# Expert stage of a hybrid encoder layer: all weight low parts on VectorE, casts on ScalarE, three pairs of gate/up banks, expert loop written out

## The chip, the cores and the metric

The kernel runs on one core of a Trainium2 chip. The metric is the device time of one execution in microseconds (us), as the median of several runs. Beside the timed runs there is one profiled execution, from which all rows below come. The core has five engines that run their own instruction lists and meet only at semaphores: PE (TensorE, matrix products), DVE (VectorE), ACT (ScalarE), POOL (GpSimd) and SP (SyncE, which here only issues DMAs).

## What is computed

One encoder layer over 1,024 prompt tokens and 256 sample tokens of width 1,024. The first part (normalisation, projections, neighbourhood attention, Fourier mixing, gated merge) is untouched. The change concerns the second part, an expert-choice feed-forward layer: each of 16 experts picks its top tokens (128 of the prompt, 32 of the sample, 160 together), applies a gated unit of width 2,048, and adds the weighted rows back.

```python
def expert_choice_ffn(h, w_router, w_gate_e, w_up_e, w_down_e):
    cap = EC_CAPACITY_FACTOR * N // N_EXPERTS
    aff = jax.nn.softmax((h @ w_router).astype(jnp.float32), axis=-1)
    gates, idx = lax.top_k(aff.T, cap)
    xe = h[idx]
    def one_expert(args):
        xc, wg, wu, wd = args
        a = xc @ wg
        b = xc @ wu
        return (jax.nn.silu(a) * b) @ wd
    ye = lax.map(one_expert, (xe, w_gate_e, w_up_e, w_down_e))
    ye = ye * gates[..., None].astype(ye.dtype)
    return jnp.zeros_like(h).at[idx.reshape(-1)].add(ye.reshape(-1, D))
```

## The kernel before

**Numbers in two parts.** To keep fp32 accuracy every fp32 operand is split into a high part (`w_hi`, `x_hl[..., 0, :]`, `act_hl[..., 0, :]`, type fp32r, written by ACT) and a low part, the difference (`w_lo` in bf16; `x_hl[..., 1, :]`, `act_hl[..., 1, :]` in fp32r). A product of weights with tokens is then `w_hi` times both parts of the tokens (320 columns: 160 high, 160 low; line 1621) plus `w_lo` times a bf16 copy of the tokens, `x_b` or `act_b` (160 columns, line 1624), summed in the same PSUM bank.

**Tiles.** Weights of an expert arrive in 12 chunks of 2 MB in four `raw` slots (line 557, issued by SP). A chunk holds two units; a unit is 2,048 numbers per partition. An expert has 24 units: 0 to 15 for gate and up, 16 to 23 for down. ACT writes the high part of a unit (line 911), then DVE or POOL its low part (`low_part`, line 459): POOL the units with v % 3 == 2 (`POOLS`, eight per expert), DVE the other sixteen (`DVES`). Six unit slots hold them. High parts run four units ahead of the products (`ahead`).

**PE's order for one expert** (the loop at line 1643): 16 gate/up tiles j, each of two half-tiles (gate, up) of 8 + 8 matmuls, into a pair of PSUM banks; then the transposes of the next expert's tokens (lines 1611 and 1612); then eight down products d of 16 + 16 matmuls, each followed by the turning back of the product before (`back`, lines 1659 and 1660); then tile 0 of the next expert, and the last turning back. Gate/up tiles alternate between two bank pairs, so tile j waits until tile j-2 has been taken out:

```python
for j in range(1, FT):
    if j >= 2:
        pe.wait_ge(gu_added, e * FT + (j - 1))
    tile_of_gate_and_up(e, j)
```

**Taking a tile out**: ACT copies the low sums from PSUM (`lows`, line 929); DVE adds them to the high sums (`gu`, line 1276, which signals `gu_added`); ACT forms `silu` (line 936); DVE multiplies (`act_f`, line 1283). For every two tiles ACT writes the high part of the result (line 940), and DVE its bf16 copy `act_b` (line 1289) and its low part (line 1291). In the down stage DVE also scales the next expert's tokens (`x_f`, line 980), casts them to `x_b` (line 1260), forms their low part (line 1264), adds `yT` (line 1298) and scales the finished rows (lines 1305 and 1306).

**POOL** also gathers the next expert's rows and adds the finished rows to the output by indirect DMAs (lines 731, 733, 760, 762).

Every engine runs its list in the order written; in the expert stage that list stands once in a loop over 16 experts, with wait values computed in registers from the loop's counter.

Of the kernel before, what the change touches and what calls it, by code (L numbers as in the profile page):

```python
# [30 lines left out]
ACT = mybir.ActivationFunctionType  # L31
# [20 lines left out]
EXPERTS, FF = 16, 2048  # L52
FT = FF // P
# [40 lines left out]

POOLS = [v for v in range(UNITS) if v % 3 == 2]
DVES = [v for v in range(UNITS) if v % 3 != 2]

# [13 lines left out]
TILES = attention_tiles()  # L111
X_BANKS = ((6, 0, 3), (7, 3, 3), (0, 6, 2))
Y_BANKS = ((1, 2), (6, 7))


def build(nc, x, g1, w_in, q_g, k_g, rpb, w_na, w_fo, w_out, g2, w_r, w_g, w_u, w_d,
          dft_c, pos_c, pos_s, spos_c, spos_s, col_mask, y):
    ctx = ExitStack()
    with ctx:
# [282 lines left out]
        hi_ready = sem("hi_ready")  # L402
        lo_dve = sem("lo_dve")
        lo_pool = sem("lo_pool")
        first_units = sem("first_units")
# [6 lines left out]
        x_hi_ready = sem("x_hi_ready")  # L412
        x_ready = sem("x_ready")
        gu_ready = sem("gu_ready")
        low_ready = sem("low_ready")
# [24 lines left out]
        def wait_split(engine, e, v):  # L440

            if v in POOLS:
                engine.wait_ge(lo_pool, e * len(POOLS) + (POOLS.index(v) + 1))
            else:
                engine.wait_ge(lo_dve, e * len(DVES) + (DVES.index(v) + 1))

# [19 lines left out]
        def _(sp):  # L466
# [130 lines left out]
            sp.wait_ge(first_units, LEAD)  # L597
            with sp.Fori(0, EXPERTS - 1) as e:
                for c in range(CHUNKS_E):
                    wait_chunk_split(e, c)  # L600
                    n = c + RAW_SLOTS
                    expert_load(e + n // CHUNKS_E, n % CHUNKS_E)
# [14 lines left out]
        def _(pool):  # L617
# [97 lines left out]

            pool.sem_inc(lo_pool, sum(v in POOLS for v in range(LEAD)))
            for v in range(LEAD):
# [18 lines left out]

            def lows(e, step):
                for v in ahead(step):
                    if v % UNITS in POOLS:
                        low_part(pool, e, v, lo_pool)  # L740

            gather(0)
            with pool.Fori(0, EXPERTS) as e:
                lows(e, 0)
                pool.wait_ge(x_tr, e + 1)
                gather(e + 1)
                for step in range(1, 4):
                    lows(e, step)
                pool.wait_ge(rows_moved, e * 64 + 64)
                pool.tensor_copy(idx_scatter[:, :], idx_t[:, :, bass.ds(e, 1)].rearrange("p a b -> p (a b)"))\  # L750
                    .then_inc(sc_count, 1)
                pool.tensor_copy(gate_now[:, :], gate_t[:, :, bass.ds(e, 1)].rearrange("p a b -> p (a b)"))\
                    .then_inc(sc_count, 1)
                pool.wait_ge(sc_count, e * 2 + 2)
                pool.sem_inc(cols_ready, 1)
                for step in range(4, 16):
                    lows(e, step)
                pool.wait_ge(y_ready, e * 4 + 5)
                apart(pool, pool_passed)
                pool.indirect_dma_start(y, bass.IndirectOffsetOnAxis(idx_scatter[:, 0:1], 0), ye_p[:, :], None,  # L760
                                        compute_op=ALU.add).then_inc(rows_moved, 16)
                pool.indirect_dma_start(y, bass.IndirectOffsetOnAxis(idx_scatter[0:CAP_S, 1:2], 0),
                                        ye_s[:, :], None, compute_op=ALU.add).then_inc(rows_moved, 16)
# [4 lines left out]
        def _(act):  # L768
# [148 lines left out]
            def token_high(n):  # L917
                act.wait_ge(xf_ready, n + 1)
                act.activation(x_hl[:, :, 0, :], x_f[:, :, :], ACT.Copy).then_inc(x_hi_ready, 1)

            token_high(0)
            with act.Fori(0, EXPERTS) as e:
                def low_sums(j):

                    b = 2 * (j % 2)
                    act.wait_ge(gu_ready, e * FT + (j + 1))
# [45 lines left out]
        def _(dve):  # L972
            dve.sem_inc(o_out, 1)
            dve.sem_inc(m_mul, 6)
            dve.sem_inc(lo_dve, sum(v in DVES for v in range(LEAD)))
            dve.sem_inc(y_ready, 1)
# [275 lines left out]
            def expert_tokens(n):  # L1252
# [15 lines left out]
            token_low(0)  # L1268
            with dve.Fori(0, EXPERTS) as e:
                def split(v):  # L1270
                    if v % UNITS in DVES:
                        low_part(dve, e, v, lo_dve)

                def add_lows(j):
                    dve.wait_ge(low_ready, e * FT + (j + 1))
                    dve.tensor_tensor(gu[j % 2][:, :, :], gate_up(2 * (j % 2))[:, :, 0:CAP], lows[j % 2][:, :, :],  # L1276
                                      ALU.add).then_inc(gu_added, 1)

                def gated_up(j):
                    dve.wait_ge(silu_ready, e * FT + (j + 1))  # L1280
                    if j >= 4 and j % 2 == 0:
                        dve.wait_ge(act_hi_ready, e * 8 + (j // 2 - 1))
                    dve.tensor_tensor(act_f[j // 2 % 2][:, j % 2, :], silu[j % 2][:, :], gu[j % 2][:, 1, :],  # L1283
                                      ALU.mult).then_inc(act_f_ready, 1)

                def act_low(pair):
                    pairs = slice(2 * pair, 2 * pair + 2)
                    dve.wait_ge(act_f_ready, e * FT + (2 * pair + 2))
                    dve.tensor_copy(act_b[:, pairs, :], act_f[pair % 2][:, :, :])  # L1289
                    dve.wait_ge(act_hi_ready, e * 8 + (pair + 1))  # L1290
# [48 lines left out]
        def _(pe):  # L1339
# [288 lines left out]
            def tile_of_gate_and_up(e, j):  # L1628
                b = 2 * (j % 2)
                for n in range(2):  # L1630
# [9 lines left out]
            pe.wait_ge(first_units, LEAD)  # L1640
            pe.wait_ge(x_ready, 1)
            tile_of_gate_and_up(0, 0)
            with pe.Fori(0, EXPERTS) as e:
# [19 lines left out]
                for d in range(KT):  # L1663
# [67 lines left out]
```

## Time and profile before

| | |
|---|---|
| time, median of 3 runs | 2791.22 us (2789.4 to 2794.93) |
| profiled execution | 2797.54 us, span 2795.7 us |
| PE busy | 2556.1 us, 91% of the span |
| DVE busy | 1766.6 us, 63% |
| ACT busy | 1250.2 us, 45% |
| POOL busy | 942.4 us, 34% |
| mean granted TensorE clock | 0.959 of full speed |

The shares mix two stages. Up to about 1,180 us DVE and POOL are lightly used; from there to the end, in the expert stage, PE and DVE are both busy some nine tenths of the time. An engine that is busy is not by that alone the one that sets the time: it has to be seen who waits for whom, and for how long.

### The profile page before, as it was taken

How to read it: one execution, taken by the hardware profiler on the slowest of the kernel's cores; microseconds unless marked ns; L12 is line 12 of the kernel's file. 1: busy time of each engine (PE TensorE's matmuls, PEld its weight loads, DVE VectorE, ACT ScalarE, POOL GpSimd, SP SyncE). 2: the span in 40 equal slices, each digit the busy share in tenths (PEclk: the TensorE clock that was granted, in tenths of full speed). 3: DMA queues.
4: the chain of work that ended last, by engine and by line, in shares of the span. 5: the costliest groups of instructions: out<-in, count | busy, mean ns of one | idle time of the engine just before them, and what ended most of it. 6: DMA issues, size and time to landing. Idle time of an engine off the chain costs nothing.

```text
span 2795.7 us, 46497 instructions
## 1 busy us (share of the span) xinstructions
PE 2556.1 (91%) x17866; PEld 2176.0 (78%) x17866; DVE 1766.6 (63%) x2096; ACT 1250.2 (45%) x1720; POOL 942.4 (34%) x364
## 2 busy tenths in 40 slices
PE   6989999999999999299999998999999999999997
PEld 5876776767767687188888888888888888889886
DVE  5114234231010233698898889889889988988986
ACT  4123333230000111166666566566666656656664
POOL 4130110101111000245445444535544554453553
PEclk7999999999999999599999999999999999999999
DMA  4240101100110153277878778778787787877872
GB/s 135 46 90 8 36 8 21 38 0 26 41 45 23 64 192 133 95 251 260 275 255 275 272 240 289 252 257 278 259 275 254 266 281 240 291 257 245 283 259 69
DMA packets 338433, 481.07 MB, mean 172 GB/s; under 512 B 22090, under 2 KB 194521, under 8 KB 338400
## 3 DMA queue, kind: packets, MB, share of 16 engines
q1 hardware_dynamic: 331072, 455.05, 48.0%
q0 software_dynamic: 7328, 25.58, 4.0%
q8 instruction: 21, 0.34, 0.1%
q14 instruction: 12, 0.10, 0.0%
HBM read 455.73 MB, written 24.87 MB: 172 GB/s over the span
## 4 chain that ended last, share of the span: by engine, by line
PE 57%; issue 24%; DVE 15%; ACT 3%; POOL 0%; DVEq 0%; DMA 0%; SPq 0%; ACTq 0%; POOLq 0%
PE ps L1343 26%; PE ps L1621 13%; PE ps L1624 6%; DVE act_f L1283 4%; PE ps L1544 4%; PE ps L1469 3%; DVE gu L1276 2%; DVE w_lo L459 2%; PE ps L1482 2%; DVE act_b L1289 1%; DVE act_hl L1291 1%; ACT w_hi L911 1%; DVE x_b L1260 1%; DVE x_f L980 1%; PE ps L1431 1%
## 5 line engine op out<-in xcount | busy, mean ns | idle before, releaser
L459 POOL TENSOR_TENSOR w_lo<-raw,w_hi 128x2048 bf16<-128x2048 f32 x132 | 643.1, 4873 | 745.7 <-ACT w_hi L911 745.4
L1621 PE MATMUL ps<-x_hl,w_hi 128*128 128x320 f32 x4112 | 746.3, 325 | 102.5 <-DVE gu L1276 97.9
L911 ACT ACTIVATE w_hi<-raw 128x2048 fp32r<-128x2048 f32 x388 | 739.3, 1906 | 3.0 <-issue 2.9
L1621 PEld LDWEIGHTS ps<-x_hl,w_hi 128*128 128x128 f32 x4112 | 620.7, 193 | 119.0 <-DVE gu L1276 71.7
L459 DVE TENSOR_TENSOR w_lo<-raw,w_hi 128x2048 bf16<-128x2048 f32 x256 | 621.1, 2426 | 79.3 <-ACT w_hi L911 79.3
L1624 PE MATMUL ps<-x_b,w_lo 128*128 128x160 bf16 x4112 | 380.8, 237 | 0.0
L1621 PE MATMUL ps<-act_hl,w_hi 128*128 128x320 f32 x2048 | 343.6, 319 | 0.0
L1624 PEld LDWEIGHTS ps<-x_b,w_lo 128*128 128x128 bf16 x4112 | 277.9, 99 | 53.8 <-issue 2.8
L1621 PEld LDWEIGHTS ps<-act_hl,w_hi 128*128 128x128 f32 x2048 | 306.2, 191 | 1.8
L1283 DVE TENSOR_TENSOR act_f<-silu,gu 128x160 f32<-128x160 f32 x256 | 290.5, 1135 | 19.4 <-ACT silu L936 19.4
L1291 DVE TENSOR_TENSOR act_hl<-act_f,act_hl 128x320 fp32r<-128x320 f32 x128 | 200.4, 1565 | 7.1 <-ACT act_hl L940 7.1
L1107 DVE TENSOR_TENSOR mT<-sig,ps 128x512 f32 (+1 forms) x24 | 14.4, 599 | 273.8 <-PE ps L1343 273.8
L929 ACT ACTIVATE lows<-ps 128x320 f32<-128x320 f32 x256 | 110.9, 433 | 142.8 <-PE ps L1624 141.3
L1624 PE MATMUL ps<-act_b,w_lo 128*128 128x160 bf16 x2048 | 171.9, 235 | 0.0
L884 ACT ACTIVATE sig<-ps 128x512 f32<-128x512 f32 (+1 forms) x48 | 25.3, 527 | 316.5 <-PE ps L1343 316.5
L1343 PE MATMUL ps<-hx_hi,w_high 128*128 128x512 f32 (+1 forms) x672 | 154.6, 373 | 7.3 <-POOL w_low L654 4.8
L936 ACT ACTIVATE silu<-gu 128x160 f32<-128x160 f32 x256 | 85.7, 335 | 160.0 <-DVE gu L1276 160.0
L1624 PEld LDWEIGHTS ps<-act_b,w_lo 128*128 128x128 bf16 x2048 | 140.3, 99 | 16.7 <-issue 0.8
L1343 PE MATMUL ps<-hx_lo,w_high 128*128 128x512 f32 (+1 forms) x672 | 142.2, 354 | 0.0
L1343 PE MATMUL ps<-hx_hi,w_low 128*128 128x512 f32 (+1 forms) x672 | 142.1, 354 | 0.0
L1343 PEld LDWEIGHTS ps<-hx_hi,w_high 128*128 128x128 f32 x672 | 114.5, 190 | 34.3 <-issue 11.1
L698 POOL CAST w_high<-m_raw 128x1024 fp32r<-128x1024 f32 x16 | 16.7, 1041 | 351.4 <-PE ps L1343 306.5
(189 smaller groups left out, 3053.5 us busy)
## 6 DMA issues: line engine op xcount, KB each, us to landing
raw<-in_w_g SPq DMA_DIRECT2D x64, 2048.0 KB, 8.1
raw<-in_w_u SPq DMA_DIRECT2D x64, 2048.0 KB, 9.9
raw<-in_w_d SPq DMA_DIRECT2D x64, 2048.0 KB, 8.4
m_raw<-in_w_in SPq DMA_DIRECT2D x16, 512.0 KB, 4.4
h_raw<-in_w_in SPq DMA_DIRECT2D x12, 512.0 KB, 4.1
x_in<-in_x SPq DMA_DIRECT2D x10, 512.0 KB, 4.1
x_res<-in_x SPq DMA_DIRECT2D x10, 512.0 KB, 4.0
y_out<-x SPq DMA_DIRECT2D x10, 512.0 KB, 2.9
```

What stands on the lines that cost most here:

```text
L459: engine.tensor_tensor(unit(w_lo, v), raw_half(v), unit(w_hi, v).bitcast(F32), ALU.subtract)\
L911: act.activation(unit(w_hi, w), raw_half(w), ACT.Copy).then_inc(hi_ready, 1)
L929: act.activation(lows[j % 2][:, :, :], gate_up(b)[:, :, CAP:2 * CAP], ACT.Copy)\
L936: act.activation(silu[j % 2][:, :], gu[j % 2][:, 0, :], ACT.Silu).then_inc(silu_ready, 1)
L1276: dve.tensor_tensor(gu[j % 2][:, :, :], gate_up(2 * (j % 2))[:, :, 0:CAP], lows[j % 2][:, :, :], ALU.add).then_inc(gu_added, 1)
L1283: dve.tensor_tensor(act_f[j // 2 % 2][:, j % 2, :], silu[j % 2][:, :], gu[j % 2][:, 1, :], ALU.mult).then_inc(act_f_ready, 1)
L1291: dve.tensor_tensor(act_hl[:, pairs, 1, :], act_f[pair % 2][:, :, :], act_hl[:, pairs, 0, :].bitcast(F32), ALU.subtract).then_inc(act_read ...
L1343: op = pe.matmul(out, lhsT, rhs, start=n == 0, stop=n == len(pairs) - 1)
L1469: op = pe.matmul(ps[:, at0:at0 + n], qkvT[part, 0, P * t:P * t + P], qkvT[part, 1, key0:key0 + n], start=True, stop=True)
L1544: op = pe.matmul(bank(2 * u + half), tokens[u][:, k, :], weights[:, k, BANK * half:BANK * half + BANK], start=k == 0 and n == 0, stop=k == ...
L1621: pe.matmul(out, unit(w_hi, v)[:, k, cols], hl[:, k, :, :].rearrange("p a n -> p (a n)"), start=k == 0, stop=False)
L1624: op = pe.matmul(out[:, CAP:2 * CAP], unit(w_lo, v)[:, k, cols], b[:, k, :], start=False, stop=k == n - 1)
```

## The change

- The low parts of all 24 units of an expert are made by DVE; POOL makes none in the loop (it still makes the first four units before it). One semaphore, `lo_ready`, takes the place of `lo_dve` and `lo_pool`.
- The bf16 copies `x_b` and `act_b` are made by ACT, right behind the high parts, in place of DVE; two new semaphores, `xb_ready` and `act_b_ready`, tell PE and DVE of them.
- Gate/up tiles go round three bank pairs (`GU_BANKS`), so tile j waits for tile j-3; the transposes and the turned rows move to other banks, and PE's wait for the finished rows of the expert before moves from ahead of the transposes to ahead of tile 2.
- The loops over the experts on all five engines are written out, so that waits are on constants.

```diff
-X_BANKS = ((6, 0, 3), (7, 3, 3), (0, 6, 2))
-Y_BANKS = ((1, 2), (6, 7))
+X_BANKS = ((6, 0, 3), (7, 3, 3), (2, 6, 2))
+Y_BANKS = ((3, 0), (6, 7))
+GU_BANKS = (0, 2, 6)
...
         def wait_split(engine, e, v):
-            if v in POOLS:
-                engine.wait_ge(lo_pool, e * len(POOLS) + (POOLS.index(v) + 1))
-            else:
-                engine.wait_ge(lo_dve, e * len(DVES) + (DVES.index(v) + 1))
+            engine.wait_ge(lo_ready, e * UNITS + (v + 1))
...
-            with sp.Fori(0, EXPERTS - 1) as e:
+            for e in range(EXPERTS - 1):
...
-            with pool.Fori(0, EXPERTS) as e:
-                lows(e, 0)
+            for e in range(EXPERTS):
                 pool.wait_ge(x_tr, e + 1)
                 gather(e + 1)
-                for step in range(1, 4):
-                    lows(e, step)
...
-                for step in range(4, 16):
-                    lows(e, step)
...
                 act.activation(x_hl[:, :, 0, :], x_f[:, :, :], ACT.Copy).then_inc(x_hi_ready, 1)
+                act.activation(x_b[:, :, :], x_f[:, :, :], ACT.Copy).then_inc(xb_ready, 1)
...
-                    b = 2 * (j % 2)
+                    b = GU_BANKS[j % 3]
...
                        .then_inc(act_hi_ready, 1)
+                    act.activation(act_b[:, 2 * pair:2 * pair + 2, :], act_f[pair % 2][:, :, :], ACT.Copy)\
+                       .then_inc(act_b_ready, 1)
...
-                dve.wait_ge(xf_ready, n + 1)
-                dve.tensor_copy(x_b[:, :, :], x_f[:, :, :])
...
                 def split(v):
-                    if v % UNITS in DVES:
-                        low_part(dve, e, v, lo_dve)
+                    low_part(dve, e, v, lo_ready)
...
-                        dve.wait_ge(act_hi_ready, e * 8 + (j // 2 - 1))
+                        dve.wait_ge(act_b_ready, e * 8 + (j // 2 - 1))
...
-                    dve.tensor_copy(act_b[:, pairs, :], act_f[pair % 2][:, :, :])
...
-                    if j >= 2:
-                        pe.wait_ge(gu_added, e * FT + (j - 1))
+                    if j == 2:
+                        pe.wait_ge(y_ready, e * 4 + 1)
+                    if j >= 3:
+                        pe.wait_ge(gu_added, e * FT + (j - 2))
                     tile_of_gate_and_up(e, j)
                 pe.wait_ge(gu_added, e * FT + (FT - 1))
-                pe.wait_ge(y_ready, e * 4 + 1)
...
                             pe.wait_ge(act_ready, e * 8 + k1 // 2)
+                            pe.wait_ge(act_b_ready, e * 8 + k1 // 2)
...
                 pe.wait_ge(x_ready, e + 2)
+                pe.wait_ge(xb_ready, e + 2)
```

What that moves on the engines is seen best in their instruction lists. First DVE at two tiles in the middle of the gate/up stage (`gu` and `act_f` take a tile out, `w_lo` is the low part of a unit, `act_hl` the low part of the result); before:

```order
L1276 TENSOR_TENSOR gu_198<-ps,lows_200 128x320
L1283 TENSOR_TENSOR act_f_196<-silu_206,gu_198 128x160
L1275 REGISTER_ALU
L1276 TENSOR_TENSOR gu_197<-ps,lows_199 128x320
L457 REGISTER_ALU
L459 TENSOR_TENSOR w_lo_187<-raw_171,w_hi_181 128x2048
L1289 CAST act_b<-act_f_196 128x320
L1290 REGISTER_ALU
L1291 TENSOR_TENSOR act_hl<-act_f_196,act_hl 128x2x160
L1283 TENSOR_TENSOR act_f_195<-silu_205,gu_197 128x160
```

and in the changed kernel:

```order
L1262 TENSOR_TENSOR gu_198<-ps,lows_200 128x320
L456 TENSOR_TENSOR w_lo_184<-raw_172,w_hi_178 128x2048
L1269 TENSOR_TENSOR act_f_195<-silu_206,gu_198 128x160
L1262 TENSOR_TENSOR gu_197<-ps,lows_199 128x320
L456 TENSOR_TENSOR w_lo_185<-raw_173,w_hi_179 128x2048
L1276 TENSOR_TENSOR act_hl<-act_f_195,act_hl 128x2x160
L1269 TENSOR_TENSOR act_f_196<-silu_205,gu_197 128x160
```

Behind every `gu` there is now a `w_lo` of DVE's own, and the cast and the register instructions are gone. Second, PE at tiles 1 to 3 (`w_hi` times `x_hl` is the high product, `w_lo` times `x_b` the low one; a wait stands behind the instruction that has it); before:

```order
L443 ISA [waits gu_added]
L1621 MATMUL ps<-x_hl,w_hi_180 128x320 [waits lo_pool]
L1621 MATMUL ps<-x_hl,w_hi_180 128x320 x7
L1624 MATMUL ps<-x_b,w_lo_186 128x160 x8
L445 REGISTER_ALU
L1621 MATMUL ps<-x_hl,w_hi_181 128x320 [waits lo_dve]
L1621 MATMUL ps<-x_hl,w_hi_181 128x320 x7
L1624 MATMUL ps<-x_b,w_lo_187 128x160 x8
L1646 REGISTER_ALU
L1621 MATMUL ps<-x_hl,w_hi_180 128x320 [waits gu_added]
```

and in the changed kernel:

```order
L1606 MATMUL ps<-x_hl,w_hi_180 128x320 [waits lo_ready,y_ready]
L1606 MATMUL ps<-x_hl,w_hi_180 128x320 x7
L1609 MATMUL ps<-x_b,w_lo_186 128x160 x8
L1606 MATMUL ps<-x_hl,w_hi_181 128x320 [waits lo_ready]
L1606 MATMUL ps<-x_hl,w_hi_181 128x320 x7
L1609 MATMUL ps<-x_b,w_lo_187 128x160 x8
L1606 MATMUL ps<-x_hl,w_hi_180 128x320 [waits gu_added]
```

Tile 2 no longer waits for `gu_added` but for the finished rows (`y_ready`); the wait for `gu_added` begins at tile 3, and it is for tile 0. The products themselves are the same.

## Rows read from the trace of the kernel before

**Rows 1.** Busy us of PE, PEld, DVE, ACT, POOL by stretch; PEclk, DMA share, GB/s

```profile
1443.57:2742.62 1299.05, 1215.44 (x10403) 1125.26 (x10401) 1150.24 (x1054) 799.47 (x949) 619.22 (x195) 0.98 0.78 264
1493.53:1499.78 6.25, 5.31 (x33) 5.01 (x34) 5.85 (x8) 3.20 (x5) 5.03 (x5) 0.73 1.00 366
```

**Rows 2.** PE's transposes (line 1611) in first and last expert: first, last start

```profile
L1611 PE MATMUL ps<-ident,xg_p x8: 273/327/328, 1245.0 to 1247.9; 128*128 128x128 f32 x8
...
L1611 PE MATMUL ps<-ident,xg_p x8: 272/328/328, 2742.6 to 2745.6; 128*128 128x128 f32 x8
```

**Rows 3.** Timeline of PE: start us, duration us, line, count, [idle before <-releaser]

```profile
1186.13 1.41 PE L1621 MATMUL ps<-x_hl,w_hi 128*128 128x320 f32 x8
...
1427.97 1.43 PE L1621 MATMUL ps<-x_hl,w_hi 128*128 128x320 f32 x8 [0.47 <-DVE gu L1276]
...
1436.90 1.42 PE L1621 MATMUL ps<-x_hl,w_hi 128*128 128x320 f32 x8
1438.16 0.73 PE L1624 MATMUL ps<-x_b,w_lo 128*128 128x160 bf16 x8
1439.95 1.43 PE L1621 MATMUL ps<-x_hl,w_hi 128*128 128x320 f32 x8 [1.06 <-DVE gu L1276]
...
1446.98 2.03 PE L1621 MATMUL ps<-act_hl,w_hi 128*128 128x320 f32 x12
...
1450.63 2.59 PE L1621 MATMUL ps<-act_hl,w_hi 128*128 128x320 f32 x16
...
1454.89 0.33 PE L1659 MATMUL ps<-ident,yT 128*128 128x128 f32 x1 [0.56 <-DVE yT L1298]
...
1455.09 2.59 PE L1621 MATMUL ps<-act_hl,w_hi 128*128 128x320 f32 x16
...
1480.97 1.42 PE L1621 MATMUL ps<-x_hl,w_hi 128*128 128x320 f32 x8
...
1494.47 1.43 PE L1621 MATMUL ps<-x_hl,w_hi 128*128 128x320 f32 x8 [2.59 <-DVE gu L1276]
```

**Rows 4.** Waits of PE, whole run: us in total, times, longest us

```profile
PE ps L1621 <- DVE gu L1276: 97.9, 80, 2.6
...
PE ps L1659 <- DVE yT L1298: 6.1, 11, 0.6
```

**Rows 5.** Timeline of POOL, then of DVE, at one of those waits

```profile
1487.94 5.82 POOL L459 TENSOR_TENSOR w_lo<-raw,w_hi 128x2048 bf16<-128x2048 f32 x1
...
1489.27 4.67 DVE L1283 TENSOR_TENSOR act_f<-silu,gu 128x160 f32<-128x160 f32 x1
```

**Rows 6.** DVE by line: ns min/median/max; page's groups: count | busy, mean ns

```profile
L1283 DVE TENSOR_TENSOR act_f<-silu,gu x256: 306/311/5248, 1189.4 to 2745.7; 128x160 f32<-128x160 f32 x128
...
L1283 DVE TENSOR_TENSOR act_f<-silu,gu 128x160 f32<-128x160 f32 x256 | 290.5, 1135 | 19.4 <-ACT silu L936 19.4
...
L1291 DVE TENSOR_TENSOR act_hl<-act_f,act_hl x128: 475/478/4848, 1199.7 to 2746.5; 128x320 fp32r<-128x320 f32 x128
...
L1291 DVE TENSOR_TENSOR act_hl<-act_f,act_hl 128x320 fp32r<-128x320 f32 x128 | 200.4, 1565 | 7.1 <-ACT act_hl L940 7.1
...
L459 DVE TENSOR_TENSOR w_lo<-raw,w_hi x256: 2268/2274/4246, 1187.2 to 2774.9; 128x2048 bf16<-128x2048 f32 x128
...
L1260 DVE CAST x_b<-x_f x17: 828/5083/5085, 1177.4 to 2748.6; 128x1280 bf16<-128x1280 f32 x17
```

**Rows 7.** ACT by line, 1,300 to 2,700 us: count | busy, mean ns

```profile
L911 ACT ACTIVATE w_hi<-raw 128x2048 fp32r<-128x2048 f32 x337 | 642.4, 1906 | 2.8 <-issue 2.8
...
L929 ACT ACTIVATE lows<-ps 128x320 f32<-128x320 f32 x225 | 97.5, 433 | 123.4 <-PE ps L1624 122.0
...
L940 ACT ACTIVATE act_hl<-act_f 128x320 fp32r<-128x320 f32 x112 | 52.4, 468 | 99.5 <-DVE act_f L1283 99.5
```

**Rows 8.** Instruction-loading queue: packets, MB, share; whole run, then 1180.26 to 1245.0 us

```profile
q8 instruction: 21, 0.34, 0.1%
...
q8 instruction: 4, 0.07, 0.4%
```

More of the change, by code:

```diff
@@ L92, in ahead @@
     return [2 * step + LEAD, 2 * step + LEAD + 1] if step < 8 else [step + 8 + LEAD]
-POOLS = [v for v in range(UNITS) if v % 3 == 2]
-DVES = [v for v in range(UNITS) if v % 3 != 2]
 def attention_tiles():
@@ L402, in build @@
         hi_ready = sem("hi_ready")
-        lo_dve = sem("lo_dve")
-        lo_pool = sem("lo_pool")
+        lo_ready = sem("lo_ready")
         first_units = sem("first_units")
@@ L413, in build @@
         x_ready = sem("x_ready")
+        xb_ready = sem("xb_ready")
+        act_b_ready = sem("act_b_ready")
         gu_ready = sem("gu_ready")
@@ L714, in _ @@
             pool.wait_ge(anti_ready, 2)
-            pool.sem_inc(lo_pool, sum(v in POOLS for v in range(LEAD)))
             for v in range(LEAD):
@@ L735, in gather @@
                     .then_inc(rows_moved, 16)
[L737 to L740, printed above, removed]
             gather(0)
-            with pool.Fori(0, EXPERTS) as e:
-                lows(e, 0)
+            for e in range(EXPERTS):
                 pool.wait_ge(x_tr, e + 1)
                 gather(e + 1)
-                for step in range(1, 4):
-                    lows(e, step)
                 pool.wait_ge(rows_moved, e * 64 + 64)
@@ L919, in token_high @@
                 act.activation(x_hl[:, :, 0, :], x_f[:, :, :], ACT.Copy).then_inc(x_hi_ready, 1)
+                act.activation(x_b[:, :, :], x_f[:, :, :], ACT.Copy).then_inc(xb_ready, 1)
             token_high(0)
-            with act.Fori(0, EXPERTS) as e:
+            for e in range(EXPERTS):
                 def low_sums(j):
-                    b = 2 * (j % 2)
+                    b = GU_BANKS[j % 3]
                     act.wait_ge(gu_ready, e * FT + (j + 1))
@@ L974, in _ @@
             dve.sem_inc(m_mul, 6)
-            dve.sem_inc(lo_dve, sum(v in DVES for v in range(LEAD)))
+            dve.sem_inc(lo_ready, LEAD)
             dve.sem_inc(y_ready, 1)
@@ L1268, in _ @@
             token_low(0)
-            with dve.Fori(0, EXPERTS) as e:
+            for e in range(EXPERTS):
                 def split(v):
-                    if v % UNITS in DVES:
-                        low_part(dve, e, v, lo_dve)
+                    low_part(dve, e, v, lo_ready)
                 def add_lows(j):
                     dve.wait_ge(low_ready, e * FT + (j + 1))
-                    dve.tensor_tensor(gu[j % 2][:, :, :], gate_up(2 * (j % 2))[:, :, 0:CAP], lows[j % 2][:, :, :],
+                    dve.tensor_tensor(gu[j % 2][:, :, :], gate_up(GU_BANKS[j % 3])[:, :, 0:CAP], lows[j % 2][:, :, :],
                                       ALU.add).then_inc(gu_added, 1)
@@ L1628, in tile_of_gate_and_up @@
             def tile_of_gate_and_up(e, j):
-                b = 2 * (j % 2)
+                b = GU_BANKS[j % 3]
                 for n in range(2):
@@ L1641, in _ @@
             pe.wait_ge(x_ready, 1)
+            pe.wait_ge(xb_ready, 1)
             tile_of_gate_and_up(0, 0)
-            with pe.Fori(0, EXPERTS) as e:
+            for e in range(EXPERTS):
                 for j in range(1, FT):
-                    if j >= 2:
-                        pe.wait_ge(gu_added, e * FT + (j - 1))
+                    if j == 2:
+                        pe.wait_ge(y_ready, e * 4 + 1)
+                    if j >= 3:
+                        pe.wait_ge(gu_added, e * FT + (j - 2))
                     tile_of_gate_and_up(e, j)
                 pe.wait_ge(gu_added, e * FT + (FT - 1))
-                pe.wait_ge(y_ready, e * 4 + 1)
                 pe.wait_ge(rows_moved, e * 64 + 64)
```

## Prediction

> **What bounds the kernel now.** I read first the busy time by stretch. In the 1,299 us from the third expert's transposes to the last one's PE is busy 94%, DVE 89%, ACT 62%, POOL 48%, and the DMA engines 78% [rows 1]. So PE is nearest to its limit, with DVE close behind, and the question is what PE does in the missing time.
>
> Then the distance of the experts: PE's transposes, once per expert, start at 1245.0 and, 15 experts later, at 2742.6 [rows 2]: 99.84 us each.
>
> Then PE's own work for one expert, from its timeline where it does not wait [rows 3]. Five half-tiles in a row take 1436.90 - 1427.97 = 8.93 us, 1.786 each, so 3.572 a tile and 57.15 for 16 tiles. The transposes end where the down products begin: 1446.98 - (1439.95 + 3.57) = 3.46. The first down product takes 1450.63 - 1446.98 = 3.65, the second 1454.89 - 0.56 of waiting - 1450.63 = 3.70. From 1455.09 to 1480.97 lie the other six, their turnings back and tile 0: 25.88 - 3.57 = 22.31. The sum is **90.27 us**, 9.57 less than the distance.
>
> Then PE's waits [rows 4]: 97.9 us in 80 waits for `gu`, five per expert, 6.1 us per expert. Each costs more than its idle time, since the next products would have begun under the tail of the last ones: 0.52 us after 1438.16 (half-tile of 1.786, less the 1.26 from 1436.90), and they began at 1439.95, 1.27 late for a wait of 1.06 [rows 3]. That is 0.2 x 5 = 1.0 us. After the longest wait (2.59 us, at 1494.47) the granted clock of the next 6.25 us is 0.73, and over the whole stretch 0.98 [rows 1, 3]; with levels of 1.2 and 2.4 GHz, 0.73 means 54% of 6.25 us at the lower one, 1.7 us lost. The wait for `yT` (11 times, 0.56 + 0.2) adds 0.5. Together 9.3 of the 9.57 us.
>
> Last, why DVE is late with `gu`. Its neighbour in the list, `act_f`, takes 0.31 us in the median but 4.67 at 1489.27, and it ends 0.2 us after a low part of POOL (1487.94 + 5.82 = 1493.76) [rows 5]. The mean is 1135 ns against a median of 311; `act_hl` 1565 against 478; the cast to `x_b` 5083 against 828 at its fastest [rows 6]. So DVE stands still while POOL subtracts, and per expert that is (1135 - 311) x 16 = 13.2, (1565 - 478) x 8 = 8.7 and 4.3: 26.2 us.
>
> **The change part by part.**
>
> *POOL's eight low parts go to DVE.* Added: 8 x 2.27 = 18.2 us per expert (the median, and within 6 ns the minimum, so this operation alone takes no longer [rows 6]). Removed: the 26.2 us of standing still, 0.83 for the `x_b` cast, and eight small casts. DVE is busy 1150.24 / 13 experts = 88.5 us now; I get 88.5 + 18.2 - 26.2 - 0.8, about 80, of 90.27: below PE. Where it is tightest, in the gate/up stage, DVE has for two tiles two low parts (4.54), two `act_f` (0.62), one `act_hl` (0.48) and two `gu` (as large as `act_hl`, 0.96): 6.6 us, while PE takes 7.14. That fits, with half a microsecond to spare per two tiles.
>
> *Casts to ACT.* `act_b` has the shape of the high part beside it, 0.47 us [rows 7]. For two tiles ACT has two high parts (3.81), two `lows` (0.87), two `silu` (smaller than `lows`, at most 0.87), and two casts of 0.47: 6.5 of 7.14 us at most. The `x_b` cast is smaller than a unit's high part (1.91); it lies in the down stage, where ACT has one high part per product of 3.7 us. No cost: its cover is ACT's idle time (62% busy [rows 1]); without it the cost would be 8 x 0.47 + 1.9 = 5.7 us per expert.
>
> *Three bank pairs.* A tile must be out by the end of the tile after next, 7.14 us after its own end, in place of 3.57. Without POOL's interference it is out, at the latest, after `lows` (0.43), a low part that DVE has just begun (2.27) and the add (0.48): 3.2 us. Two pairs would just do; with three nearly 4 us are in hand. So all five waits per expert go, with the clock's fall behind the longest of them. What is late next: `yT` of the first down product, behind which PE waits 0.56 now. In its path the 5.1 us `x_b` cast goes and a low part of 2.27, which must wait for ACT's high part, comes in. From the end of the last tile (T): `lows`, `gu`, `silu`, `act_f` and the last high part of the result, 0.43 + 0.48 + 0.43 + 0.31 + 0.47 = 2.1 us, or 4.4 if a low part stands ahead; then `act_b` 0.47, the unit's high part 1.91, its low part 2.27, three `x_f` of together some 1.7 (estimate: twice the fastest `x_b`, which has as many elements) and `yT` 0.31: T + 8.8 to T + 11.1. PE asks for it at T + 3.46 + 3.65 + 3.70 = T + 10.8. Mostly in time: I count this wait as gone, and up to 0.5 us per expert in the range.
>
> *The wait for the finished rows moves* to tile 2. Queued behind it are all later tiles; behind the last turning back PE has tile 1 (3.57 us) to do, while DVE scales two pieces of 512 columns (1.7 us by the fastest `x_b`, which has 1,280). No cost. PE's new waits on `act_b` and `x_b` end with casts that ACT makes beside DVE's low part of the same numbers.
>
> *The loop written out.* Of the 22.31 us above, six down products of 3.65 leave 0.4 for seven turnings back and the loop's end together [rows 3], so the loop costs PE at most that, 6 us in all; I take nothing. In its place about 28,700 instructions of PE are loaded in place of 4,700. Now 21 packets bring 0.34 MB in the whole run [rows 8]; then some 127. In the first expert four came in while PE went from tile 1 at 1186.13 to its transposes at 1245.0, 58.87 us: 5.3 above its 15 tiles' 53.58, where the mean expert loses 9.57. Loading is hidden there. I take nothing; the price, if not, is a rival.
>
> The Trainium skill's page "Runtime: NRT & Kernel Launch", section "Instruction fetch mechanics", says that a taken branch out of the window at hand stalls until the target has been fetched, which is why full unrolling is preferred. By it the written-out loop would bring a gain of its own at each of 15 loop ends, one fetch long; by the row it is at most 0.4 us each. The sum is 2642 by the row and could be 2636 by the rule.
>
> *DMA.* 0.78 x 99.84 = 77.9 us of transfers per expert [rows 1]; 90.27 us hold them, at 86%.
>
> *Sum.* First expert, from tile 1 to the transposes: 5.3. Fifteen distances: 15 x 9.57 = 143.6. The last down stage: 0.7 for its `yT`. Together **149.6 us**, which makes the profiled 2797.5 a 2647.9; the median of the runs is 6.3 us (0.2%) below the profiled run, so I forecast 2791.2 - 149.6 = **2642 us**.
>
> **The rivals.**
>
> *PE keeps waiting a little for DVE.* DVE's reserve is half a microsecond in two tiles and less at the first `yT`; the in-order lists of ACT and DVE hang on each other, and a hiccup of one is worked off slowly. For: the thin sums above. Against: the third bank pair. A microsecond per expert is 16 us, three are 48: 2658 to 2690.
>
> *DVE is not freed.* If its long `act_f` have another cause than POOL, it has 88.5 + 18.2 - 5.1 for `x_b`, less eight small casts (0.48 at most), 98 to 102 us per expert, as many as PE has now: no change, about 2790. Against: the end of the long one falls on POOL's [rows 5].
>
> *Slower: instruction loading.* The 106 further packets come through DMA engines that are then 86% busy. If each holds up PE for 1.4 us, the 149.6 us are gone, and beyond that the kernel is slower: at 3 us each, 2642 + 318 = 2960. For: nothing in this trace loads code steadily beside such traffic. Against: the first expert [rows 8].
>
> *Slower: ACT and DVE in step.* If DVE's low part kept ACT from the next tile, a tile would take 0.43 + 1.91 + 2.27 + 0.31 = 4.92 us; it decides from (99.84 - 33.1) / 16 = 4.2. At 4.92 an expert takes 111.8: about 2985. Against: in ACT's list nothing waits for `w_lo`.
>
> **How the numbers follow.** PE without waits, 2632 to 2652: 0.80. Small waits left, up to 2690: 0.12. No change: 0.02. Loading: 0.04. In step: 0.02. The range reaches over the first two, 2632 to 2690. A measurement tells about 0.2% from no change; faster 0.92, same 0.02, slower 0.06.
>
> **What would show it.** Transposes every 90.3 us; PE's wait for `gu` gone; granted clock 1.0 in the expert stage; means of `act_f` and `act_hl` at their medians; DVE some 80 us per expert. Wrong if PE idles at regular places with no engine as releaser (loading), if `yT` of the first down product shows on PE, or if DVE's low parts take more than 2.27 us: from 2.27 + (90.27 - 80) / 24 = 2.7 us each DVE is the bound.

## The result and the profile after

The changed kernel takes 2660.9 us (median of 4 runs, 2658.1 to 2664.1) beside 2791.6 us for the kernel before: a ratio of 0.953, with a 95% interval of 0.951 to 0.954. On another chip, with five runs, it was 2659.8 us, and 0.951 (0.950 to 0.952). The forecast was 2642, the range 2632 to 2690. The sign and most of the size are right; 19 us of the forecast gain are missing. Two executions far outside the others, one of the kernel before (3119.3 us) and one of the closer mixture below (6312.6 us), are left out of all ratios.

The profiled execution took 2658.06 us. First its busy time by engine, then the expert stage by stretch, from the first expert's transposes to the last one's (columns as in [rows 1]):

```profile
PE 2520.9 (95%) x17866; PEld 2159.3 (81%) x17866; DVE 1558.9 (59%) x2079; ACT 1302.0 (49%) x1865; POOL 419.3 (16%) x236
```

```profile
1238.50:2602.60 1364.10, 1364.10 (x12003) 1277.53 (x12001) 1130.67 (x1201) 970.17 (x1230) 232.55 (x105) 0.99 0.88 292
```

PE is busy for all of the 1364.1 us, where it had 94% before [rows 1]. DVE has 1130.67 / 15 = 75.4 us per expert, where it had 88.5, though it makes eight more low parts.

Of the waits [rows 4] nothing is left. From the first expert's first product to the end, PE's list has one row, the start of the stage, which the kernel before had too:

```profile
PE ps L1606 <- DVE x_hl L1251: 4.6, 1, 4.6
```

DVE by line, 1,330 to 2,580 us (count, busy us, mean ns, idle before), which answers to [rows 6]:

```profile
L456 DVE TENSOR_TENSOR w_lo<-raw,w_hi 128x2048 bf16<-128x2048 f32 x329 | 751.5, 2287 | 159.3 <-ACT w_hi L897 158.7
...
L1269 DVE TENSOR_TENSOR act_f<-silu,gu 128x160 f32<-128x160 f32 x218 | 69.1, 317 | 5.6 <-ACT silu L923 5.6
L1276 DVE TENSOR_TENSOR act_hl<-act_f,act_hl 128x320 fp32r<-128x320 f32 x109 | 52.9, 485 | 8.5 <-ACT act_hl L927 8.5
```

The means of `act_f` and `act_hl` are now where their medians were: 317 ns for 1135, 485 for 1565.

The chain of work that ended last, once 57% PE and 24% "issue", is PE alone, and code is loaded in 116 packets in place of 21 [rows 8]:

```profile
PE 93%; DVE 3%; issue 1%; ACT 1%; POOL 1%; DMA 0%; SPq 0%; DVEq 0%; ACTq 0%; POOLq 0%
...
q8 instruction: 116, 1.90, 0.3%
```

If PE never waits, where are the missing 19 us? The transposes, which answer to [rows 2], lie 90.2 us apart in eight of the 15 distances and 91.7 or 91.8 in seven. Three of them in a row of experts (first and last start in us):

```profile
L1596 PE MATMUL ps<-ident,xg_p x8: 273/327/328, 1509.2 to 1512.1; 128*128 128x128 f32 x8
...
L1596 PE MATMUL ps<-ident,xg_p x8: 272/327/328, 1599.4 to 1602.4; 128*128 128x128 f32 x8
...
L1596 PE MATMUL ps<-ident,xg_p x8: 273/327/328, 1691.1 to 1694.1; 128*128 128x128 f32 x8
```

The first distance is 90.2, the second 91.7. By stretch (PEclk is the third last column): the transposes at 1599.4, the 5.2 us behind them, and the same place one expert earlier:

```profile
1599.40:1602.81 3.41, 3.41 (x19) 2.11 (x16) 2.56 (x5) 1.19 (x4) 0.00 (x0) 0.99 0.95 319
1602.81:1608.00 5.19, 5.19 (x34) 4.78 (x33) 3.43 (x4) 2.22 (x3) 0.00 (x0) 0.68 1.01 375
1509.20:1515.00 5.80, 5.80 (x38) 4.40 (x37) 3.19 (x7) 3.41 (x5) 0.00 (x0) 1.00 1.00 346
```

Behind the transposes of some experts the granted clock is 0.68, with no idle time of PE before: between the levels of 1.2 and 2.4 GHz that is 64% of 5.19 us at the lower one, 1.7 us lost, and a whole expert that is 1.5 us longer. All seven long experts have this fall, in this place (0.67 to 0.71); the others do not (1.00). Why these seven and not the others is open.

### The profile page after: what moved, and what is told of

The parts are those of the page before. It is cut to its first block, busy times and chain, and to the rows that moved or that the text cites. A ratio compares the mean times of both kernels' runs of the same rounds, so it can differ in the third digit from the quotient of the medians.

```text
span 2656.3 us, 44107 instructions
## 1 busy us (share of the span) xinstructions
PE 2520.9 (95%) x17866; PEld 2159.3 (81%) x17866; DVE 1558.9 (59%) x2079; ACT 1302.0 (49%) x1865; POOL 419.3 (16%) x236
## 4 chain that ended last, share of the span: by engine, by line
PE 93%; DVE 3%; issue 1%; ACT 1%; POOL 1%; DMA 0%; SPq 0%; DVEq 0%; ACTq 0%; POOLq 0%
PE ps L1606 35%; PE ps L1328 27%; PE ps L1609 17%; PE ps L1529 4%; PE ps L1454 3%; PE ps L1467 2%; PE ps L1596 1%; PE ps L1597 1%; PE ps L1416 1%; PE ps L1646 1%; PE ps L1647 1%; PE ps L1374 0%; DVE top_i L1212 0%; DVE aff L1214 0%; DVE top_v L1211 0%
## 5 line engine op out<-in xcount | busy, mean ns | idle before, releaser
L456 DVE TENSOR_TENSOR w_lo<-raw,w_hi 128x2048 bf16<-128x2048 f32 x384 | 877.2, 2287 | 186.8 <-ACT w_hi L897 186.2
L1606 PE MATMUL ps<-x_hl,w_hi 128*128 128x320 f32 x4112 | 730.2, 320 | 4.6 <-DVE x_hl L1251 4.6
L1606 PEld LDWEIGHTS ps<-x_hl,w_hi 128*128 128x128 f32 x4112 | 607.8, 189 | 5.1 <-issue 4.7
L1609 PE MATMUL ps<-x_b,w_lo 128*128 128x160 bf16 x4112 | 374.1, 234 | 0.0
L1609 PEld LDWEIGHTS ps<-x_b,w_lo 128*128 128x128 bf16 x4112 | 272.2, 98 | 52.7 <-issue 0.2
L746 POOL DMA_INDIRECT y_out<-ye_p,idx_scatter x16 | 83.1, 5196 | 1105.4 <-DVE ye_s L1291 1105.4
L1328 PEld LDWEIGHTS ps<-hx_lo,w_high 128*128 128x128 f32 x672 | 113.4, 190 | 18.0
L1328 PEld LDWEIGHTS ps<-hx_hi,w_low 128*128 128x128 f32 x672 | 113.0, 189 | 17.5
L1262 DVE TENSOR_TENSOR gu<-ps,lows 128x320 f32<-128x320 f32 x256 | 123.3, 482 | 5.7 <-ACT lows L916 5.7
L936 ACT ACTIVATE y_low<-ps 128x160 f32<-128x160 f32 x128 | 38.9, 304 | 178.3 <-PE ps L1609 178.3
```

Of the source, the lines that this page charges most:

```text
L456: engine.tensor_tensor(unit(w_lo, v), raw_half(v), unit(w_hi, v).bitcast(F32), ALU.subtract)\
L936: act.activation(y_low[d % 2][:, :], bank(4 + d % 2, CAP, first=CAP), ACT.Copy)\
L1262: dve.tensor_tensor(gu[j % 2][:, :, :], gate_up(GU_BANKS[j % 3])[:, :, 0:CAP], lows[j % 2][:, :, :], ALU.add).then_inc(gu_added, 1)
L1328: op = pe.matmul(out, lhsT, rhs, start=n == 0, stop=n == len(pairs) - 1)
L1606: pe.matmul(out, unit(w_hi, v)[:, k, cols], hl[:, k, :, :].rearrange("p a n -> p (a n)"), start=k == 0, stop=False)
L1609: op = pe.matmul(out[:, CAP:2 * CAP], unit(w_lo, v)[:, k, cols], b[:, k, :], start=False, stop=k == n - 1)
```

## The experiments

Eleven runs tell three things apart: which of the four parts of the change brought the gain, why POOL's work had cost so much, and what the remaining 1.5 us are. The ratios are against the kernel before on the same chip: its median is 2795.1 us beside the changed kernel once more, the run without the written-out loop, the one with two bank pairs and the transposes laid between; 2794.6 beside the runs with all low parts on DVE, with three bank pairs and with idle work on POOL; 2793.8 beside the casts on ACT, the closer mixture and the two things together.

### The changed kernel once more

> The changed kernel once more, beside the runs below on the same chip, as the level that they are held against. The theory: PE alone sets the time of an expert (90.24 us of its own work in the trace of the changed kernel, and no waits), and in 7 of 15 experts 1.5 us more at a lower granted clock right behind the transposes. Expected: 2661 us, within 4, and again some experts at 90.2 and some at 91.7 us.

Measured: 2659.8 us (2653.5 to 2662.0), ratio 0.951 (0.950 to 0.952); seven experts again at 91.7 or 91.8 us, the same seven in the order of experts, and eight at 90.2.

### The change without the written-out loop

```diff
-            for e in range(EXPERTS):
+            with pe.Fori(0, EXPERTS) as e:
                 for j in range(1, FT):
```

and likewise on the other four engines.

> The changed kernel with its five expert loops put back as loops. Theory (the loop's end costs PE at most 0.4 us per expert): 2661 to 2667 us, and only one expert's code loaded. Rival (a branch back costs the fetch of its target, so writing out the loop was part of the gain): a gap on PE at each of 15 loop ends, of 1 us or more, 2676 us and above. A second rival (the steady loading of code costs the changed kernel something): below 2655 us.

Measured: 2661.3 us, ratio 0.952 (0.951 to 0.953), the same as the change. PE has no gap at a loop's end, and 21 packets load code in the whole run in place of 116. The written-out loop neither brings nor costs anything that can be measured.

### The change with two bank pairs

```diff
-                b = GU_BANKS[j % 3]
+                b = GU_BANKS[j % 2]
...
-                    if j == 2:
-                        pe.wait_ge(y_ready, e * 4 + 1)
-                    if j >= 3:
-                        pe.wait_ge(gu_added, e * FT + (j - 2))
+                    if j >= 2:
+                        pe.wait_ge(gu_added, e * FT + (j - 1))
```

with `GU_BANKS = (0, 2)`, `X_BANKS` and `Y_BANKS` as before, and the wait for the finished rows ahead of the transposes again.

> The changed kernel with two pairs of gate/up banks as before. Theory (POOL's low parts held up DVE, and without them a tile is out 3.2 us after its end, with 3.57 allowed): 2661 to 2672 us, no more than small waits of PE for gu. Rival (the third pair is what freed PE): PE's waits for gu come back, five per expert at 1 us or more, 2735 us and above.

Measured: 2657.1 us, ratio 0.951 (0.949 to 0.952). PE does not wait once in the expert stage. With all low parts on DVE the third pair is not needed.

### The kernel before, with all low parts on DVE and nothing else

```diff
-POOLS = [v for v in range(UNITS) if v % 3 == 2]
-DVES = [v for v in range(UNITS) if v % 3 != 2]
+POOLS = []
+DVES = list(range(UNITS))
...
-            pool.sem_inc(lo_pool, sum(v in POOLS for v in range(LEAD)))
```

> The kernel before, with one thing changed: DVE makes all 24 low parts, POOL none. Casts stay on DVE, two bank pairs, the loop stays. Theory (DVE stood still while POOL subtracted): act_f and act_hl fall to 0.31 and 0.48 us in the mean, DVE has 88.5 + 18.2 - 26.2 = 80.5 us per expert, PE 90.3; little waiting is left: 2661 to 2700 us. Rival (the third bank pair or the casts are needed for the gain, DVE has too much to do): PE's waits for gu stay at several us per expert, 2740 us and above.

Measured: 2660.2 us, ratio 0.952 (0.950 to 0.955): the whole gain of the change, with two bank pairs, the casts on DVE and the loop. PE has no waits, and the cast that took 5.1 us is back at its fastest (DVE by line, 1,330 to 2,580 us):

```profile
L1282 DVE TENSOR_TENSOR act_f<-silu,gu 128x160 f32<-128x160 f32 x217 | 68.5, 316 | 5.6 <-ACT silu L935 5.6
...
L1259 DVE CAST x_b<-x_f 128x1280 bf16<-128x1280 f32 x14 | 11.6, 827 | 0.5
```

DVE has as many low parts to make as in the changed kernel, and the casts besides, and is still busy for only 1069.87 us of 1,250, PE for all of them:

```profile
1330.00:2580.00 1250.00, 1250.00 (x10961) 1170.72 (x10961) 1069.87 (x1218) 840.42 (x996) 232.40 (x98) 0.99 0.86 289
```

### The kernel before, with three bank pairs and nothing else

```diff
-                    b = 2 * (j % 2)
+                    b = GU_BANKS[j % 3]
...
-                    if j >= 2:
-                        pe.wait_ge(gu_added, e * FT + (j - 1))
+                    if j == 2:
+                        pe.wait_ge(y_ready, e * 4 + 1)
+                    if j >= 3:
+                        pe.wait_ge(gu_added, e * FT + (j - 2))
...
-                pe.wait_ge(y_ready, e * 4 + 1)
```

with the bank tables of the change, and the same `b` where ACT and DVE take a tile out.

> The kernel before, with one thing changed: three pairs of gate/up banks. POOL keeps its eight low parts, the casts stay on DVE, the loop stays. Theory: DVE still stands still 26 us per expert, but its 88.5 us are under PE's 90.3, so with 7.14 us in place of 3.57 to take a tile out most of the waits for gu are hidden, the one for yT stays (0.76 us): 2680 to 2740 us. Rival (standing still costs PE whatever the banks allow, since the low parts come late too): 2780 us and above. Rival the other way (the third pair alone is the gain): 2665 us or below.

Measured: 2811.0 us, ratio 1.007 (1.005 to 1.008), a little slower than before. My theory (2740 at the most) missed; the time is in the range of the first rival (2780 and above), but not for its reason: for low parts that come late PE waits 3.2 us in the whole stage. PE's waits from 1,180 us on (us in total, times, longest us; line 1612 is a transpose, 1622 a tile):

```profile
PE ps L1612 <- DVE gu L1277: 61.9, 16, 3.9
PE ps L1622 <- DVE gu L1277: 30.1, 31, 1.5
PE ps L1622 <- POOL w_lo L460: 3.2, 15, 0.2
```

Between the tiles the third pair does what it is for: 30 us of waits in place of 98 [rows 4]. But DVE is no faster for it. It falls behind over the whole gate/up stage, and the transposes behind the last tile, which wait for tile 14's `gu`, then stand for all of it at once, 3.9 us in each expert. My expectation had taken DVE's 88.5 us of the whole expert against PE's 90.3. The stage decides. In one gate/up stage up to the transposes, with PE at 52.66 us, DVE has work or stands for 56.72 of 58.70:

```profile
1385.50:1444.20 58.70, 52.66 (x466) 48.71 (x465) 56.72 (x52) 37.68 (x51) 33.11 (x12) 1.00 0.89 296
```

More buffers hide a lateness that comes and goes, not one that adds up.

PE's waits are 95 us together, 9 less than before [rows 4], and the kernel is 16 us slower even so. What PE loses besides is clock: behind the long wait in each expert come the small transposes, and the granted clock is low there, 0.65 over 9.8 us in the expert below. From the third expert's transposes to the last one's it is 0.96, where it was 0.98 [rows 1]; 0.02 of some 1,300 us is 26 us.

```profile
1443.00:2752.00 1309.00, 1229.76 (x10400) 1131.39 (x10400) 1154.42 (x1056) 791.71 (x951) 628.86 (x195) 0.96 0.78 263
1444.20:1454.00 9.80, 9.80 (x49) 7.46 (x49) 9.16 (x12) 3.17 (x5) 3.35 (x1) 0.65 0.99 356
```

One of DVE's stops in this kernel, POOL's instruction and DVE's:

```profile
1435.40 4.61 POOL L460 TENSOR_TENSOR w_lo<-raw,w_hi 128x2048 bf16<-128x2048 f32 x1 [6.63 <-ACT w_hi L912]
1435.58 4.61 DVE L1290 CAST act_b<-act_f 128x320 bf16<-128x320 f32 x1
```

The victim here is the small cast, which was never held in the kernel before (327 ns at the most): whichever such instruction comes next while POOL subtracts.

### The kernel before, with the casts on ACT and nothing else

```diff
                 act.activation(x_hl[:, :, 0, :], x_f[:, :, :], ACT.Copy).then_inc(x_hi_ready, 1)
+                act.activation(x_b[:, :, :], x_f[:, :, :], ACT.Copy).then_inc(xb_ready, 1)
...
                 op.then_inc(xf_ready, 1)
-                dve.wait_ge(xf_ready, n + 1)
-                dve.tensor_copy(x_b[:, :, :], x_f[:, :, :])
...
                     dve.wait_ge(act_f_ready, e * FT + (2 * pair + 2))
-                    dve.tensor_copy(act_b[:, pairs, :], act_f[pair % 2][:, :, :])
```

and `act_b` on ACT behind its high part, with the waits of the change.

> The kernel before with one thing changed: the casts to x_b and act_b on ACT. POOL keeps its low parts, two bank pairs, the loop stays. Theory: the 5.1 us of x_b leave DVE in the down stage, where PE waits 0.76 us for yT in 11 of 16 experts; in the gate/up stage another two-operand instruction of DVE meets POOL's low parts, so PE's five waits for gu stay: 2770 to 2795 us. Rival (the casts were what made DVE late): below 2740 us.

Measured: 2796.4 us, ratio 1.001 (1.000 to 1.002): nothing, and 1 us above the range of my theory. The cast `x_b` has left DVE, and the next instruction takes its place as the victim. First DVE's low part of the tokens, 1.48 us when it is alone, then PE's waits:

```profile
L1267 DVE TENSOR_TENSOR x_hl<-x_f,x_hl 128x1280 fp32r<-128x1280 f32 x13 | 73.4, 5645 | 0.0
```

```profile
PE ps L1623 <- DVE gu L1279: 76.9, 66, 2.6
PE ps L1662 <- DVE yT L1300: 28.9, 16, 1.9
```

The waits for `gu` are fewer (97.9 before), those for `yT` more (6.1 before).

### The changed kernel, with idle work on POOL

Two kernels give POOL work again at the eight places per expert where it had made low parts. It goes to a buffer of its own that nobody reads. The first subtracts, from two SBUF operands; the second only fills.

```diff
+                        for n in range(3):
+                            pool.wait_ge(junk_done, count[0])
+                            pool.tensor_tensor(junk[:, :, :], src, src, ALU.subtract).then_inc(junk_done, 1)
```

```diff
+                        for n in range(6):
+                            pool.wait_ge(junk_done, count[0])
+                            pool.memset(junk[:, :, :], 0.0).then_inc(junk_done, 1)
```

> The changed kernel, and POOL given work again that nobody needs: at the eight places per expert where it made low parts, three subtractions of 640 numbers each from two SBUF operands, written to a buffer of its own. Theory (POOL's subtractions hold DVE's two-operand instructions): act_f and act_hl are in the mean well above 0.31 and 0.48 us again, DVE has 75 + some 20 to 25 us per expert, over PE's 90.2, and PE waits again: 2720 to 2830 us. Rival (the long DVE instructions had another cause, such as the weights' own low parts on POOL reading the raw slots): act_f at 0.31 us, 2661 us.

Measured: 2869.4 us in a single run, 75 above the kernel before. POOL's and DVE's groups and PE's waits:

```profile
L743 POOL TENSOR_TENSOR junk<-ident 128x640 bf16<-128x640 f32 x384 | 811.7, 2114 | 610.2 <-ACT w_hi L915 587.7
```

```profile
L457 DVE TENSOR_TENSOR w_lo<-raw,w_hi 128x2048 bf16<-128x2048 f32 x288 | 754.5, 2623 | 78.0 <-ACT w_hi L915 78.0
L1287 DVE TENSOR_TENSOR act_f<-silu,gu 128x160 f32<-128x160 f32 x192 | 142.7, 743 | 4.8 <-ACT silu L941 4.8
...
L1294 DVE TENSOR_TENSOR act_hl<-act_f,act_hl 128x320 fp32r<-128x320 f32 x96 | 84.2, 877 | 7.3 <-ACT act_hl L945 7.3
```

```profile
PE ps L1614 <- DVE gu L1280: 60.7, 15, 4.6
PE ps L1624 <- DVE gu L1280: 48.2, 35, 2.3
PE ps L1664 <- DVE yT L1301: 26.0, 15, 1.7
```

Work on data that has nothing to do with the weights makes PE wait at all three places, the tiles, the transposes and `yT`; `act_f` is at 743 ns for 317. So the raw slots and the semaphores of the low parts were not the cause. It cost more than I expected (2830 at the most): a subtraction of 640 took 2.1 us, three of them 6.3 at each place, where one low part had taken 4.9.

> As the run before, but POOL fills the buffer (six fills of 640 numbers at each place) and reads nothing. If only POOL work that reads SBUF holds DVE, as the Trainium skill's page on SBUF has it for DVE instructions with two SBUF operands: act_f at 0.31 us, about 2661 us. If any POOL work does: act_f above 0.31 us in proportion to the time of the fills, 2670 us and above.

Measured: 2662.9 us in a single run, as the changed kernel. POOL is busy 882 us in all, more than twice the 419 of the changed kernel, and DVE does not notice (the page's group of POOL, then DVE by line):

```profile
L742 POOL MEMSET junk<- 128x640 bf16 x768 | 493.1, 642 | 640.6 <-ACT w_hi L914 602.1
```

```profile
L1286 DVE TENSOR_TENSOR act_f<-silu,gu 128x160 f32<-128x160 f32 x216 | 68.4, 317 | 5.6 <-ACT silu L940 5.6
```

Of the two kinds of work on POOL, the one that reads SBUF holds DVE and the one that only writes it does not; that it is the reading, and not another difference between a subtraction and a fill, these two runs alone do not show. The Trainium skill's page "SBUF — State Buffer", section "Who interferes with whom", says this: a DVE instruction with two SBUF inputs contends with a GpSimd instruction that reads SBUF, not with one that only writes it, and the later one waits out the whole of the earlier. Both runs agree (743 ns against 317), and so does `gu`, which has one operand in PSUM and was at 477 ns beside POOL's subtractions. By the runs two inputs are not needed, though: the casts read one operand, in SBUF, and were held as well, `x_b` for 5083 ns in place of 828 [rows 6] and `act_b` in the run with three bank pairs.

### The transposes laid between the first down product's matmuls

```diff
                 for k in part:
                     pe.matmul(out, unit(w_hi, v)[:, k, cols], hl[:, k, :, :].rearrange("p a n -> p (a n)"),
                               start=k == 0, stop=False)
+                    if between and k % GAP == GAP - 1:
+                        between.pop(0)()
...
-                expert_transposes()
+                between = transpose_pairs()
```

`between` holds the eight pairs of transposes; with `GAP = 3` one pair follows every third of the first 24 matmuls. It is given to the first down product alone.

> The changed kernel with the 16 transposes of an expert laid between the first 24 matmuls of the first down product, two behind every third one, in place of all ahead of it. Theory (the 3.4 us of small transposes in a row are what lets the granted clock fall behind them): no expert at 91.7 us, 7 x 1.5 us = 10 us gained, about 2650 us, granted clock of the expert stage 1.00. Rival (the clock falls as often or more, since the thin stretch is now 6 us long): 2661 us or above. Second rival (the next expert's tokens come 2.7 us later and DVE is late with yT or the token's low part): PE waits for yT in each expert, up to 2690 us.

Measured: 2643.7 us (2643.2 to 2644.2), ratio 0.946 (0.945 to 0.947), faster than the change. The first and the last of its 15 distances' ends, and the whole stretch:

```profile
L1605 PE MATMUL ps<-ident,xg_p x8: 270/272/273, 1237.1 to 1242.2; 128*128 128x128 f32 x8
...
L1605 PE MATMUL ps<-ident,xg_p x8: 270/272/273, 2589.8 to 2595.0; 128*128 128x128 f32 x8
```

```profile
1238.50:2580.00 1341.50, 1341.50 (x11904) 1252.69 (x11905) 1120.00 (x1189) 962.06 (x1218) 226.81 (x105) 1.00 0.89 294
```

(2589.8 - 1237.1) / 15 = 90.18 us, no expert above 90.2, granted clock 1.00. The five runs also lie within 1 us, where those of the changed kernel spread over 6 and 8. The granted clock of each run of the changed kernel goes with its time: 0.966 in the fastest (2653.5 us), 0.962 in the slowest (2662.0) of the second chip; here it is 0.969 or 0.970 in all five. That fits a number of falls that differs from run to run, but the falls were counted in profiled runs alone. Of the 18.7 us between the two profiled runs on this chip, 11.4 lie in the 15 distances and 1.9 behind the last transposes; 5.9 lie ahead of the first transposes, where the edit changes nothing, and are not explained.

### The same, more closely

The same kernel with `GAP = 1`: one pair behind each of the first eight matmuls.

> The changed kernel with the transposes laid in between more closely: one pair behind each of the first eight matmuls of the first down product, so that the whole stretch is some 5 us in place of 6. If any large matmul between the transposes keeps the clock up: no expert at 91.7 us, 2644 us, as with one pair behind every third matmul. If it is the share of large matmuls in the stretch that counts: some experts at 91.7 us again, 2647 to 2661 us.

Measured: 2651.5, 2653.4 and 2659.6 us, ratio 0.951 (0.948 to 0.953). Thirteen distances are at 90.6, two at 93.6. One of the two by stretch: 5.2 us in which the transposes begin (at 1506.1), and the 7.8 us behind, in which they end:

```profile
1503.40:1508.60 5.20, 5.20 (x39) 4.09 (x39) 4.16 (x8) 3.07 (x6) 0.00 (x0) 1.00 1.03 361
1508.60:1516.40 7.80, 7.80 (x37) 5.89 (x37) 4.55 (x6) 2.63 (x3) 0.00 (x0) 0.57 0.75 267
```

So a large matmul between the transposes does not by itself keep the clock: with three between two pairs no fall was seen, with one there were two. The falls are rarer than with all transposes in a row, and each is longer. Why every expert is 0.4 us longer than with `GAP = 3` was not followed up.

### The two things that count, on the kernel before

All low parts on DVE and the transposes laid between with `GAP = 3`; two bank pairs, casts on DVE, the loop.

> The kernel before with two things changed: DVE makes all low parts, and the transposes are laid between the first matmuls of the first down product. Casts on DVE, two bank pairs, the loop stays. Theory (POOL's low parts and the clock's fall behind the transposes were all that PE lost): 90.2 us per expert in every expert, about 2644 us, as the changed kernel with the transposes laid in between (2643.67). Rival (with everything tight, two pairs and the casts on DVE cost something once the tokens come 2.7 us later): PE waits for yT or gu, 2650 to 2680 us.

Measured: 2644.4 us (2643.8 to 2647.1), ratio 0.947 (0.945 to 0.949); every distance 90.2 us, PE without a wait. It needs two edits in place of the change's four, and lies 149 us under the kernel before on its chip, where the changed kernel lay 135 under it on another.

## Why the prediction was right, and where it fell short

- **PE's own work per expert, 90.27 us**: right. The undisturbed distances after are 90.2 us, and 90.18 in the mean where no clock falls.
- **DVE stands still while POOL subtracts**: right. All low parts on DVE gives the whole gain alone; needless subtractions on POOL bring the waits back. DVE's sum was forecast at about 80 us per expert and is 75.4. The forecast named the eight small casts but did not take them off (8 x 0.31 = 2.5 us), and it left out that DVE's own low parts stood still too, with a mean of 2426 ns beside the median of 2274: 16 x 0.15 = 2.4 us.

```profile
L459 DVE TENSOR_TENSOR w_lo<-raw,w_hi 128x2048 bf16<-128x2048 f32 x256 | 621.1, 2426 | 79.3 <-ACT w_hi L911 79.3
```

- **Casts to ACT at no cost**: right, and they bring nothing either (1.001 alone; the changed kernel without them, as the run with all low parts on DVE, is as fast).
- **Two pairs would just do**: right, 2657.1 us. The thin reserve at the first `yT` held as well: PE waits for it nowhere.
- **The written-out loop**: right at zero. The Trainium skill's page "Runtime: NRT & Kernel Launch", section "Instruction fetch mechanics", which the prediction weighed, has a stall for a taken branch whose target must be fetched first. No run here shows one: with the loop put back there is no gap at its end, and the 21 packets of the whole run leave no fetch for each round. Steady loading of code beside DMA engines at 88% costs nothing either; that rival is out.
- **The clock: a loss that the sum put at nothing.** The prediction took the lower granted clock for a consequence of the longest wait and let all 1.7 us per expert go with it. That fall did go. There was a second kind, which could be read in the trace of the kernel before: behind the transposes that begin at 1542.9 the clock is 0.72, with PE busy throughout; its last wait, of 1.07 us, had ended at 1539.3. Four more of the 15 experts have a fall there.

```profile
1545.00:1551.00 6.00, 6.00 (x34) 5.22 (x34) 5.35 (x9) 2.61 (x3) 2.37 (x1) 0.72 1.00 355
```

  I had looked at one expert, and in that one the fall came at the wait. In the changed kernel seven of 15 experts have a fall behind the transposes, 7 x 1.5 = 10.5 us, and the expert stage has 0.99, where the forecast wanted 1.0.
- **From the profiled run to the median.** Between the two profiled executions the change is 2797.5 - 2658.1 = 139.5 us; forecast were 149.6. The 10.1 us are the seven falls: the 15 distances are 1364.1 us, and 15 x 90.27 is 1354.05. The other 9 of the 19 us come from the translation: the profiled run before lay 6.0 us above its median (2791.6), the one after lies 2.9 below its own (2660.9). With falls that come in some experts and some runs, a single profiled run was no measure to a few microseconds.
- **The rivals**: small waits left, DVE not freed, code loading and ACT and DVE in step are all out, by PE's empty list of waits.
- **The range: right in part by luck.** For PE without waits, the case that came, the forecast had 2632 to 2652, and 2660.9 lies above it. It lies in the band that was added for small waits of PE (2658 to 2690), and there are none. The range held because that band was wide enough for two other things, the falls of the clock and the single profiled run.

## What to carry to other kernels

Before a second engine is given half of a job, look at whether the two hold each other: compare an instruction's mean with its median, and lay the long ones beside the other engine's timeline; moving or buffering the victims (the casts, the third bank pair) brought nothing, taking away the holder brought all. Judge whether an engine keeps up by the stage in which it has most to do, not by the whole round. And when PE no longer waits, look at its granted clock behind stretches of small products, and lay such products between large ones, loosely: here one pair behind every third large product kept the clock, one behind every one did not always.

## What was not expected of the hardware

- Subtractions on POOL hold DVE's instructions that read SBUF alone, until the subtraction has ended, and make the sum worse than no help: eight low parts, 8 x 2.27 = 18.2 us on DVE, cost DVE 26.2 us of standing still per expert when POOL made them (the prediction's sum from [rows 6]). With an operand in PSUM, as in `gu`, none was held, and beside fills none at all (`act_f` 327 ns at the most).
- The granted clock falls without PE having been idle: behind the 16 transposes in a row it did so in seven of 15 experts, at 1.5 us each; with one pair between every three matmuls it did so in none of the 30 distances of two kernels.
- DVE holds POOL as well: the indirect DMA that adds the rows takes POOL 5.4 us to issue in the median after the change, and 3.2 before. Before, one low part of DVE runs beside it, after, two in a row, and each time it ends 1.5 us behind them; beside none, in the last expert, it takes 1.6 us. Nobody waits for it here.

```profile
1367.92 5.44 POOL L746 DMA_INDIRECT y_out<-ye_p,idx_scatter  x1 [66.11 <-DVE ye_s L1291]
...
1367.40 4.47 DVE L456 TENSOR_TENSOR w_lo<-raw,w_hi 128x2048 bf16<-128x2048 f32 x2
```
